# A two-layer float32 model on one core: retention scores of two heads issued together, and the next weight unit split ahead of the long branch's SiLU

## The reference, cut to what matters

```python
qh, kh = rotary(q), rotary(k) * 64 ** -0.5          # 4 heads of 64
o_n    = sum_{m<=n} gamma_h ** (n - m) (q_n . k_m) v_m   # retention, v: 4 heads of 128
y_ret  = (silu(g_ret) * head_groupnorm(o)) @ w_ret_out[l]
y_sc   = (sc_b * causal_dwconv(sc_c * sc_x, 3 taps)) @ w_sc_out[l]
c      = causal_dwconv(cf_a * sigmoid(cf_b), 31 taps)
y_cf   = silu(layernorm(c)) @ w_cf_out[l]           # the long branch
merged = gates[0] * y_ret + gates[1] * y_sc + gates[2] * y_cf
x      = x + rmsnorm(merged @ w_o[l])
```

## Time and profile before

| | us |
|---|---|
| median of 3 executions | 3086.61 (3086.41 to 3092.4) |
| the profiled execution: its own time | 3090.3 |
| its span, first to last instruction | 3088.2 |
| PE busy | 2929.7 (95%) |
| DVE busy | 2016.4 (65%) |
| ACT busy | 1278.5 (41%) |
| mean granted TensorE clock | 0.973 of 2.4 GHz |

### The profile page before, as it was taken

One profiled execution on the slowest core, in us unless ns is written; L12 is line 12 of the kernel. 1 busy time (PEld: TensorE's weight loads), 2 busy tenths in 40 slices (PEclk: granted clock), 3 DMA queues, 4 the chain that ended last, 5 costly groups with the idle time before them and its releaser, 6 DMA issues. The chain is left out here.

```text
span 3088.2 us, 33494 instructions
## 1 busy us (share of the span) xinstructions
PE 2929.7 (95%) x12948; PEld 2343.4 (76%) x12948; DVE 2016.4 (65%) x2451; ACT 1278.5 (41%) x1522; POOL 338.3 (11%) x109
## 2 busy tenths in 40 slices
PE   5899889989989889999999999999999999999999
PEld 5447766767778777778877878888888787888887
DVE  7685699968778648996567746665047676366631
ACT  4542667744311147785213234444142223254422
POOL 0201000000000000000000000444400000024442
PEclk8898899989999989999999999999999999999999
DMA  6143499933200018994322222222333222322222
GB/s 252 56 158 142 170 411 412 359 121 103 89 28 14 28 55 293 342 375 155 115 82 85 92 96 96 96 95 99 115 107 109 77 87 90 115 82 95 95 96 89
DMA packets 92114, 430.45 MB, mean 139 GB/s; under 512 B 10246, under 2 KB 14759, under 8 KB 65352
## 3 DMA queue, kind: packets, MB, share of 16 engines
q1 hardware_dynamic: 88136, 401.29, 36.0%
q10 hardware_dynamic: 3840, 27.27, 2.3%
HBM read 424.32 MB, written 2.10 MB: 138 GB/s over the span
## 5 line engine op out<-in xcount | busy, mean ns | idle before, releaser
L241 PE MATMUL psum<-h_high,weights_low 128*128 128x512 f32 x1792 | 704.8, 393 | 5.9 <-DVE h_low L370 4.6
L242 PE MATMUL psum<-h_high,weights_high 128*128 128x512 f32 x1792 | 701.2, 391 | 0.0
L243 PE MATMUL psum<-h_low,weights_high 128*128 128x512 f32 x1792 | 701.1, 391 | 0.0
L183 ACT ACTIVATE weights_high<-weights_raw 128x2048 fp32r<-128x2048 f32 x162 | 310.0, 1914 | 704.6 <-PE psum L243 683.2
L187 POOL TENSOR_TENSOR weights_low<-weights_raw,weights_high 128x2048 fp32r<-128x2048 f32 x68 | 314.0, 4617 | 2169.1 <-ACT weights_high L183 2169.1
L370 DVE TENSOR_TENSOR weights_low<-weights_raw,weights_high 128x2048 fp32r<-128x2048 f32 (+1 forms) x102 | 224.8, 2208 | 432.6 <-ACT weights_high L183 238.1
L241 PEld LDWEIGHTS psum<-h_high,weights_low 128*128 128x128 f32 x1792 | 338.3, 189 | 85.1 <-issue 13.3
L243 PEld LDWEIGHTS psum<-h_low,weights_high 128*128 128x128 f32 x1792 | 338.2, 189 | 71.9
L242 PEld LDWEIGHTS psum<-h_high,weights_high 128*128 128x128 f32 x1792 | 338.2, 189 | 70.7 <-issue 0.5
L1688 DVE TENSOR_TENSOR weights_low<-more_raw,weights_high 128x1024 fp32r<-128x1024 f32 x168 | 203.4, 1224 | 16.9 <-ACT weights_high L1343 14.5
L1688 DVE TENSOR_TENSOR weights_low<-weights_raw,weights_high 128x1024 fp32r<-128x1024 f32 x168 | 201.5, 1222 | 11.0 <-ACT weights_high L1343 8.8
(11 more groups left out here) (469 smaller groups left out, 4722.1 us busy)
## 6 DMA issues: line engine op xcount, KB each, us to landing
weights_raw<-in_moe SPq DMA_DIRECT2D x168, 512.0 KB, 5.7
more_raw<-in_moe SPq DMA_DIRECT2D x168, 512.0 KB, 5.7
weights_raw<-in_w_mix SPq DMA_DIRECT2D x76, 1024.0 KB, 4.8
weights_raw<-in_w_ffn SPq DMA_DIRECT2D x66, 1024.0 KB, 4.8
mod_weights<-in_ada_w SPq DMA_DIRECT2D x32, 512.0 KB, 3.6
q_nope_then_x_tokens<-in_ada_w ACTq DMA_DIRECT2D x16, 1024.0 KB, 8.2
weights_raw<-in_hy_w_in SPq DMA_DIRECT2D x12, 1024.0 KB, 5.0
mod_weights<-in_ada_w SPq DMA_DIRECT2D x8, 1024.0 KB, 21.6
```

Source lines behind the costliest of these rows:

```text
L183: self.nc.scalar.activation(self.high[:, g % 2, :], self.raw[:, g % 2, :], ACT.Copy).then_inc(self.high_done, 1)
L241: nc.tensor.matmul(out, w[1], rhs[0], start=start, stop=False)
L242: nc.tensor.matmul(out, w[0], rhs[0], start=False, stop=False)
L243: return nc.tensor.matmul(out, w[0], rhs[1], start=False, stop=stop)
```

## The change

Heads are issued in pairs (0 and 1, then 2 and 3). `scores(t, i)` issues tile i of both heads of pair t, one behind the other, to two adjacent banks. The waits and the places of `outs`, the decays and the copies follow that:

| behind unit | before | after |
|---|---|---|
| 9 | scores of head 0 | tiles 0, 1 of pair 0 |
| 10 | outs 0, scores of head 1 | tiles 2, 3 of pair 0 |
| 11 | outs 1, scores of head 2 | tile 0 of pair 1, outs 0, outs 1 |
| 12 | outs 2, scores of head 3 | tiles 1, 2, 3 of pair 1 |
| 13 | outs 3 | outs 2, outs 3 |

Separately, ACT's wait for `cf_scaled`, the four SiLU pieces and the write of `branch_high` move from the end of step 27 into step 28, behind the high part of unit 30 and ahead of the sigmoid of step 28.

```diff
-        score_at = ((4, 0), (5, 0), (6, 0), (5, S - P))
+        score_at = ((4, 0), (6, 0), (4, 0), (4, 2 * P))
-        def score(i):
+        def score(h, i):
             b, at = score_at[i]
-            return m.psum[:, b, at:at + S - i * P]
+            return m.psum[:, b + h % 2, at:at + S - i * P]
...
+            def scores(t, i):
+                for h in (2 * t, 2 * t + 1):
+                    side = slice(64 * (h % 2), 64 * (h % 2) + 64)
+                    nc.tensor.matmul(score(h, i), m.raw[side, RAW_K + t, i * P:(i + 1) * P],
+                                     m.raw[side, RAW_Q + t, i * P:S], start=True, stop=True).then_inc(s.scores, 1)
             def outs(h):
-                pe.wait_ge(s.decayed, TT * (h + 1))
-                if h:
-                    pe.wait_ge(s.copied, h)
+                pe.wait_ge(s.decayed, 2 * TT * (h // 2 + 1))
                 for i in range(TT):
-                    mm = nc.tensor.matmul(m.psum[:, 7, i * P:S], vr[:, i, h * P:(h + 1) * P],
+                    mm = nc.tensor.matmul(m.psum[:, 6 + h % 2, i * P:S], vr[:, i, h * P:(h + 1) * P],
...
-                if 10 <= u <= 13:
-                    outs(u - 10)
-                if 9 <= u <= 12:
-                    scores(u - 9)
+                if u == 9:
+                    scores(0, 0)
+                    scores(0, 1)
+                if u == 10:
+                    pe.wait_ge(s.decayed, 2)
+                    scores(0, 2)
+                    scores(0, 3)
+                if u == 11:
+                    pe.wait_ge(s.decayed, 2 * TT)
+                    scores(1, 0)
+                    outs(0)
+                    outs(1)
+                if u == 12:
+                    pe.wait_ge(s.copied, 2)
+                    scores(1, 1)
+                    pe.wait_ge(s.decayed, 2 * TT + 2)
+                    scores(1, 2)
+                    scores(1, 3)
+                if u == 13:
+                    outs(2)
+                    outs(3)
...
# ACT
+                if u == 28:
+                    act.wait_ge(s.cf_scaled, 1)
+                    (the four SiLU pieces, act.wait_ge(s.cf_silu, 4), the write of Bh: as they were)
-                if 10 <= u <= 13:
-                    h = u - 10
-                    act.wait_ge(s.outs, h + 1)
-                    nc.scalar.activation(OR[:, h, :], m.psum[:, 7, :], ACT.Copy).then_inc(s.copied, 1)
+                if u in (11, 13):
+                    for h in (u - 11, u - 10):
+                        act.wait_ge(s.outs, h + 1)
+                        nc.scalar.activation(OR[:, h, :], m.psum[:, 6 + h % 2, :], ACT.Copy).then_inc(s.copied, 1)
...
# DVE
+            def decayed(t, i):
+                for h in (2 * t, 2 * t + 1):
+                    dve.wait_ge(s.scores, 2 * TT * t + (2 * i + h % 2 + 1 if i < 2 else 2 * TT))
+                    tt(ST[:, h % 2, i, 0:S - i * P], score(h, i), dec[:, h, 0:S - i * P], ALU.mult).then_inc(s.decayed, 1)
+                if w == 10:
+                    (waits for s.here and s.qk as before) decayed(0, 0), decayed(0, 1)
+                if w == 11:
+                    decayed(0, 2), decayed(0, 3)
+                if w == 12:
+                    dve.wait_ge(s.outs, 2)
+                    decayed(1, 0)
+                if w == 13:
+                    for i in range(1, TT):
+                        decayed(1, i)
```

More of the change, by code:

```diff
@@ L2443, in _ @@
                     ring.make_high(act, u + 2)
+                if u == 28:
+                    act.wait_ge(s.cf_scaled, 1)
+                    for c in range(4):
+                        nc.scalar.activation(ca[:, c, :], ca[:, c, :], ACT.Silu, scale=m.param("cf_g", 1, 4 * layer + c),
+                                             bias=m.param("cf_lb", 1, 4 * layer + c)).then_inc(s.cf_silu, 1)
+                    act.wait_ge(s.cf_silu, 4)
+                    nc.scalar.activation(Bh[:, :, :], ca, ACT.Copy).then_inc(s.b_high, 1)
                 if u in (0, 1):
@@ L2483, in _ @@
                         .then_inc(s.cf_root, 1)
[L2484 to L2489, removed]
                 if u == 31:
@@ L2585, in _ @@
                     tt(qk, ST[:, 0, :, :], ST[:, 1, :, :], ALU.add).then_inc(s.qk, 1)
[L2586 to L2595, removed]
+                if w == 10:
+                    dve.wait_ge(s.here, 16)
+                    dve.wait_ge(s.qk, 1)
+                    decayed(0, 0)
+                    decayed(0, 1)
+                if w == 11:
+                    decayed(0, 2)
+                    decayed(0, 3)
+                if w == 12:
[4 more added lines that the diff above has]
+                        decayed(1, i)
                 if w == 12:
```

## The result

The changed kernel took 3069.36 us (median; 3066.93 to 3073.05) against 3087.16 for the kernel before beside it: a ratio of 0.994, interval 0.9926 to 0.9955. The prediction was 3070.3, with a range of 3066.5 to 3076.5.

What follows compares the result with a forecast made beforehand. PE, busy 95% of the span, was taken as the bound: give it less work or remove a wait. Terms -8.3, -6.5 and -1.5 make -16.3 us, from the 3086.6 median to 3070.3; range 3066.5 to 3076.5.

Steps and rivals of the forecast that it cites:

- Part 1, the pairs: Retention bursts behind units 9 to 12: the second head of each pair's scores is free, -8.3 us, bounds 0 and -8.3.
- the one taken over from quarters to halves: Score matmuls: four row quarters behind unit 16 were seen streaming at once, and the same was assumed for two halves.
- 2.07 us for a head: Price of one head's 8 passes, 2560 columns, read from the outs behind unit 13; 0.81 ns a column.
- The 0 for the changes of tiling: Units 9 to 12: still four bursts a layer, each changing tiling at 0.28 us, so no gain or loss.
- The waits beside it: Units 9 to 13: no new PE wait costs anything; DVE loses about 1 us in step 12, covered by 7.39 and 6.42 idle.
- Rival D: DVE's step 12, waiting for two outs, delays unit 14's low part and becomes the bound: about 3090 us, slower; chance 0.03.
- Rival A: Score bursts: passes start in program order, so only neighbours of different heads overlap; 2.7 us less gain, 3073.0 us; chance 0.09.
- Part 2, the SiLU: Unit 30's first matmul: its wait for branch_low goes, 3.27 us a layer, -6.5 us; bounds -6.5 and -4.5.
- the forecast's 1802.95: Layer one: predicted end of DVE's branch_low, letting PE start unit 30 at 1803.0, with only 0.1 us to spare.
- Rival C: SiLU chain before unit 30 is no shorter, so the wait goes only partly; at worst 3078.3 us; chance 0.06.
- The clock: Second layer behind unit 30's wait: the fall to half clock goes along with the idle time, -1.5 us.
- the bound of -3.1: Clock term's far bound: in other executions both layers may have had the fall to half clock.

Runs made afterwards that it cites:

- e1: Changed kernel with the SiLU pieces and the write of branch_high back in step 27, so the head pairs alone: 3079.32 us against 3087.26, ratio 0.9974.
- e4: Changed kernel with heads paired (0, 2) and (1, 3), so both tiles of a pair lie in the same 64 rows: 3079.11 us in one run.
- e3: Changed kernel with all tiles of the even head issued before all of the odd head inside each burst: 3074.81 us in one run.
- e5: Changed kernel with the SiLU pieces and the write of branch_high behind the sigmoid of step 28 instead of ahead of it: 3076.35 us in one run.
- e2: Kernel before with only the SiLU pieces and the write of branch_high moved to step 28, behind unit 30's high part: 3078.03 us, ratio 0.9969.
- e8: Changed kernel with attention's probability transposes one tile later, four probability buffers and a fourth score bank, without pairing halves there: 3064.16 us in one run.
- e9: The changed kernel run again with nothing edited, to measure the attention's own scatter: 3067.95 us, ratio 0.9939.
- e10: Changed kernel with attention's 64-feature score parts paired across halves, transposes one tile later and value products one more tile later: 3054.27 us against 3087.46, ratio 0.989.
- e6: Changed kernel with attention's 64-feature score parts issued for two query tiles at once in different halves, four score banks: 3074.75 us against 3087.26, ratio 0.9954.
- e7: Changed kernel with attention's 64-feature score parts paired across halves, transposes one tile later and four probability buffers: 3070.97 us, ratio 0.9948.

## Why the prediction was right

**What bounds.** PE at 95% and two ways to win: both held. From unit 9 of the first layer on, the two profiled executions differ by 21.3 - 4.4 = 16.9 us, and the three parts below are all of it.

**Part 1, the pairs.** Forecast -8.3, measured 2 x 4.31 = -8.6 us from unit 9 to unit 14, and 7.9 by e1's median. The step that could have failed was the one taken over from quarters to halves; e4 shows that the halves are the whole of it. What was off is the size of a term: 2.07 us for a head is too little by 0.09. The burst behind unit 13 ends beside a unit, whose first matmul takes 1623.60 - 1623.28 = 0.32 us to the next start instead of the usual 0.23, and that part of the price wasn't counted. In the kernel before, the unit's second matmul:

```profile
1623.60 0.39 PE L242 MATMUL psum<-h_high,weights_high 128*128 128x512 f32 x1
```

In the changed kernel two outs follow each other there, and the second starts 1612.48 - 1610.33 = 2.15 us behind the first, 0.84 ns a column (both in one row, then the second alone):

```profile
1610.33 4.48 PE L2333 MATMUL psum<-scores,v_tok_then_gated 128*128 128x512 f32 x16
1612.48 2.32 PE L2333 MATMUL psum<-scores,v_tok_then_gated 128*128 128x512 f32 x8
```

In e4 a pass of 512 columns on 64 rows takes 0.43 us to the next one's start, 0.84 ns a column too. Two heads a layer at 2.15 are the 4.3 us that went. The 0 for the changes of tiling held.

**The waits beside it.** No new wait of PE for a decay or a copy is on the list. DVE did wait in step 12 for the second outs, 1.25 us where about 1 was counted, and was idle for 7.30 and 2.99 us before the low parts that were named as its cover. In the changed kernel's timeline of DVE:

```profile
1587.00 1.29 DVE L2535 TENSOR_TENSOR scores<-psum,merged 128x512 f32<-128x512 f32 x2 [1.25 <-PE psum L2333]
...
1599.94 2.29 DVE L370 TENSOR_TENSOR weights_low<-weights_raw,weights_high 128x2048 fp32r<-128x2048 f32 x1 [7.30 <-ACT weights_high L183]
...
1612.62 2.29 DVE L370 TENSOR_TENSOR weights_low<-weights_raw,weights_high 128x2048 fp32r<-128x2048 f32 x1 [2.99 <-ACT weights_high L183]
```

The second cover is less than half of the 6.42 that it was the earlier trace rows: PE's gap behind unit 12 is 3.1 us shorter, and step 13 has six decays (2.07 us) where it had four (1.68). Rival D had the right place, and its price was never reached.

**Rival A and the rule.** Behind unit 9 two passes start together and the burst is 1.71 us long, where A has 1.73 + 0.41, so A is out in the changed kernel. e3 goes further. The Trainium skill ("TensorE: Matmul & The Clock Gate", Part 3) has matmuls start in program order; in e3 a pass in the other half started 13 ns behind the first one, with three earlier ones still waiting. For matmuls in different row halves the measurement decides against the rule. e3 also bounds its opposite: four passes of one half in a row cost nothing, six cost 0.8 us.

**Part 2, the SiLU.** Forecast -6.5. From unit 29's last matmul to unit 30's first it is 0.23 us instead of 3.50, in both layers: -6.5 for both, and -6.8 from one unit's end to the next, the clock left out. Each step of the chain came as written, even the table load behind the high part. The changed kernel's DVE scaling ends 8.7 us earlier than before; taken off the forecast's 1802.95, the end of `branch_low` would be 1794.25, and it was 1794.27. The spare was 0.16 us, where 0.1 was said. Rival C is out by the same rows. e5 shows how narrow the place is: behind the sigmoid instead of ahead of it, 4.2 of the 6.2 us return.

**The clock.** Forecast -1.5, measured -1.5: from unit 29's last matmul to unit 30's it was 16.05 us in layer two before, 14.57 in layer one, and both are 11.19 now. e1 shows that the bound of -3.1 was rightly kept: with the same two waits the clock fell behind both (16.1 and 17.1 us from unit 29's last matmul to unit 30's), as its window in layer two shows:

```profile
2609.00:2616.00 7.00, 5.72 (x14) 4.47 (x15) 3.43 (x2) 1.75 (x2) 0.00 (x0) 0.51 0.78 263
```

**The sum.** -8.6, -6.8 and -1.5 are -16.9 us, against -16.3 forecast. The profiled pair differs by 21.3; the other 4.4 lie ahead of the end of unit 9 of the first layer, where no instruction was changed. There the granted clock differs between the two executions, in one stretch by this much (before, then after):

```profile
1040.00:1180.00 140.00, 124.64 (x596) 107.22 (x595) 68.59 (x139) 54.81 (x66) 14.87 (x7) 0.88 0.19 66
```
```profile
1040.00:1180.00 140.00, 124.15 (x617) 105.89 (x616) 74.11 (x146) 58.18 (x70) 14.95 (x7) 0.93 0.22 78
```

e1, e2, e8 and e9 have 0.93 there as well, e10 has 0.88. The forecast had found the profiled execution of before 3.7 us above its median; those are most of the 4.4. Against the medians, 17.8 us apart, the sum is 1 us short, within what two sets of runs differ by. What set off the lower clock in the profiled execution of before is open. The parts came as forecast; that the median came within 1 us of it is in part luck, as the four executions of the changed kernel lie 6.1 us apart.

## What to carry to other kernels

Matmuls that fill only half of the array's rows came in twos for the price of one when their data lay in different halves, here always with tiles in different banks (one bank for both was not run) and with no more than four passes of one half in a row. In the retention, where PE waited for nothing, this was the whole gain, and it can be counted in columns beforehand, with a price a column that is read where two bursts of the same kind follow each other. Where the engine's stream is bound to a chain on other engines instead (e6), the same saving turned into waits until both readers behind it, the transposes and the value products, were put a tile later (e10). And a block of another engine's work is best put where that engine was idle, with every queue ahead of it written out: here the place within one step was worth 2 us a layer (e5).

## What was not expected of the hardware

Passes of different halves don't start in the order of issue (e3): up to three waiting ones were passed over, and in the row behind unit 16, with quarters, too. A wait of PE of 2 to 3 us is followed by half clock in some cases and not in others: of two such waits one in the kernel before, two in e1, one in e5, at a price of 1.5 to 2.6 us each. What decides it isn't shown. And e7 and e10 differ by one move of the value products, with what reads them, and by 16.7 us of median: with two waits in one chain, taking away the first showed nothing until the second was gone.
